# First halves of the first two projection units placed among the second-half modulation products, which use another PSUM bank

## The reference

```python
mod = c @ w_ada + b_ada                                  # c: one prompt row, 8 sample rows
shift, scale, gate = jnp.split(mod[:, None, :], 3, axis=-1)
h = rms_norm(x, norm_g) * (1 + scale) + shift            # (tokens, 1024)
proj = h @ w_in                                          # 3328 columns, split in eight
...                                                      # window attention; HGRN2 recurrence
g_a, g_b = jnp.split(jax.nn.sigmoid(h @ w_merge + b_merge), 2, axis=-1)
y = g_a * (ya @ w_proj_a) + g_b * (yb @ w_proj_b)
out = x + gate * (y @ w_out)
```

## Time and profile before

| | us |
|---|---|
| device time, median of 3 runs | 1617.27 |
| lowest, highest | 1616.54, 1617.92 |
| the profiled execution's own time | 1617.43 |
| its span, first to last instruction | 1614.5 |
| TensorE busy in it | 1564.4 (97%) |
| VectorE, ScalarE, GpSimd busy | 752.2, 555.2, 822.6 |

### The profile page before, as it was taken

One profiled execution on the slowest core, in us unless ns is written; L12 is line 12 of the kernel. 1 busy time (PEld: TensorE's weight loads), 2 busy tenths in 40 slices (PEclk: granted clock), 3 DMA queues, 4 the chain that ended last, 5 costly groups with the idle time before them and its releaser, 6 DMA issues.

```text
span 1614.5 us, 32929 instructions
## 1 busy us (share of the span) xinstructions
PE 1564.4 (97%) x13608; PEld 1268.2 (79%) x13608; DVE 752.2 (47%) x1930; ACT 555.2 (34%) x1131; POOL 822.6 (51%) x1080
## 2 busy tenths in 40 slices
PE   5999999999999999999999999999999999999998
PEld 2787778877888778888879877788888977788886
DVE  3665554233458655532245665623334655623122
ACT  3334323434322432333422343244432344143330
POOL 2425333556673633455756452437777363337671
PEclk9999999999999999999999999999999999999999
DMA  9723112344565321233365331223455331123351
GB/s 321 230 77 93 54 55 66 92 120 129 170 164 124 102 77 51 70 93 117 92 184 132 85 92 54 67 72 115 137 174 156 86 105 54 55 79 91 93 163 67
DMA packets 304971, 175.87 MB, mean 109 GB/s; under 512 B 74158, under 2 KB 290567, under 8 KB 304808
## 3 DMA queue, kind: packets, MB, share of 16 engines
q1 hardware_dynamic: 304824, 173.79, 37.3%
HBM read 159.69 MB, written 11.96 MB: 106 GB/s over the span
## 4 chain that ended last, share of the span: by engine, by line
PE 88%; DVE 6%; issue 2%; ACT 2%; SPq 2%; DMA 1%; POOL 0%; DVEq 0%
PE ps_D L751 50%; PE ps_D L748 24%; PE ps_XD L806 2%; SPq L503 2%; ACT p_or_hf L1107 1%; PE ps_XB L885 1%; PE ps_XA L918 1%; PE ps_XA L907 1%; PE ps_XB L933 1%; PE ps_XA L938 1%; PE ps_XB L932 1%; DMA th_t<-in_w_ada 1%; DVE p_or_hf L1462 1%; PE ps_XC L818 1%; PE ps_XA L885 1%
## 5 line engine op out<-in xcount | busy, mean ns | idle before, releaser
L1650 POOL TENSOR_TENSOR w_lo_t<-w_raw,w_hi_t 128x256 fp32r<-128x256 f32 x928 | 676.9, 764 | 632.1 <-ACT w_hi_t L964 631.8
L751 PE MATMUL ps_D<-h_hi_t,w_hi_t 128*128 128x512 f32 x1024 | 414.9, 405 | 0.1
L751 PE MATMUL ps_D<-h_hi_t,w_lo_t 128*128 128x512 f32 x1024 | 400.4, 391 | 1.2 <-issue 1.2
L751 PE MATMUL ps_D<-h_lo_t,w_hi_t 128*128 128x512 f32 x1024 | 400.8, 391 | 0.0
L964 ACT ACTIVATE w_hi_t<-w_raw 128x1024 fp32r<-128x1024 f32 x232 | 240.2, 1052 | 78.8 <-PE ps_D L748 45.0
L751 PEld LDWEIGHTS ps_D<-h_hi_t,w_hi_t 128*128 128x128 f32 x1024 | 193.0, 188 | 51.9 <-issue 14.8
L751 PEld LDWEIGHTS ps_D<-h_hi_t,w_lo_t 128*128 128x128 f32 x1024 | 192.8, 188 | 42.0
L751 PEld LDWEIGHTS ps_D<-h_lo_t,w_hi_t 128*128 128x128 f32 x1024 | 193.2, 189 | 36.3 <-issue 0.3
L748 PE MATMUL ps_D<-w_hi_t,h_hi_t 128*128 128x384 f32 (+1 forms) x384 | 141.9, 370 | 3.0 <-issue 1.4
L748 PE MATMUL ps_D<-w_hi_t,h_lo_t 128*128 128x384 f32 (+1 forms) x384 | 136.4, 355 | 1.5 <-issue 1.5
L748 PE MATMUL ps_D<-w_lo_t,h_hi_t 128*128 128x384 f32 (+1 forms) x384 | 136.4, 355 | 0.0
(11 more groups left out here) (390 smaller groups left out, 2373.5 us busy)
## 6 DMA issues: line engine op xcount, KB each, us to landing
w_raw<-in_w_in SPq DMA_DIRECT2D x72, 512.0 KB, 3.9
w_raw<-in_w_merge SPq DMA_DIRECT2D x64, 512.0 KB, 4.0
w_raw<-in_w_in SPq DMA_DIRECT2D x64, 256.0 KB, 3.9
w_raw<-in_w_out SPq DMA_DIRECT2D x32, 512.0 KB, 4.1
x_or_AT<-in_x_prompt SPq DMA_DIRECT2D x20, 512.0 KB, 5.2
w_raw<-in_w_proj_a SPq DMA_DIRECT2D x64, 128.0 KB, 3.0
w_raw<-in_w_proj_b SPq DMA_DIRECT2D x32, 256.0 KB, 3.2
xr<-in_x_prompt SPq DMA_DIRECT2D x16, 512.0 KB, 4.8
```

What stands on the lines that cost most here:

```text
L751: ins = mm(bank[:, :], w[:, s0, k0 + k, :], a[:, k, :], start=go, stop=end)
L1650: ins = g_.tensor_tensor(w_lo[:, c, k:k + 2], w_raw[:, n % NRAW, k:k + 2], f32(w_hi[:, c, k:k + 2]), ALU.subtract)
```

## The change

Parts 0 and 1 of the second half of the modulation products stay where they are. Then comes half 0 of unit 0, part 2, half 0 of unit 1, and part 3. The loop over units leaves these two halves out; its side work stays. Because half 0 of unit 1 writes bank D1, the modulation products of the second half that wrote D1 now write XC. XC held the turned sample rows, so these are copied to `hS` first (one new instruction on VectorE), and TensorE waits for the copy (`p_hS`) ahead of the second half. No product is added or taken away.

```diff
-            def ada_half(h):
-                for p in range(4):
+            def ada_part(h, parts):
+                for p in parts:
...
-                    for n, b in (((0, "D0"), (2, "XC")), ((1, "D1"), (3, "XD")))[h]:
+                    for n, b in (((0, "D0"), (2, "XC")), ((1, "XC"), (3, "XD")))[h]:
...
-            ada_half(0)
+            ada_part(0, range(4))
...
             s.wait_ge("p_vec", 1)
-            ada_half(1)
-            s.wait_ge("p_rows", 4)
-            turn_rows(1)
+            s.wait_ge("p_hS", 1)
...
+            ada_part(1, (0, 1))
+            dense(0, 0, 0)
+            ada_part(1, (2,))
+            dense(0, 1, 0)
+            ada_part(1, (3,))
+            s.wait_ge("p_rows", 4)
+            turn_rows(1)
             for it in range(NIT):
                 for u in range(NU):
                     for hf_ in (0, 1):
-                        dense(it, u, hf_)
+                        if it or u > 1 or hf_:
+                            dense(it, u, hf_)
...
-            s.done(fn(mod_rows[:, 512:1024], pb["D1"][:, :], ACT.Copy), "p_rows")
+            s.done(fn(mod_rows[:, 512:1024], XC[:, :], ACT.Copy), "p_rows")
...
+            s.wait_ge("p_T", 3)
+            do(cp(hS[:, :, 0:NS], XC[:, 0:NS * KT].rearrange("p (k b) -> p k b", k=KT)), "p_hS")
             modulation(0)
...
-            do(tt(hS[:, :, 0:NS], XC[:, 0:NS * KT].rearrange("p (k b) -> p k b", k=KT), gscale[:, :, 0:NS],
-                  ALU.mult))
+            do(tt(hS[:, :, 0:NS], hS[:, :, 0:NS], gscale[:, :, 0:NS], ALU.mult))
```

More of the change, by code:

```diff
@@ L247 @@
         + [f"ada{k}" for k in range(2 * KT)] + [f"gw{p}" for p in range(4)]
-        + ["p_late", "p_load0", "p_load1", "p_load2", "p_load3", "p_load4", "p_c", "p_T", "p_xs", "p_mod", "hm", "p_vec", "p_lb", "p_exp0", "p_rows", "p_scale", "p_x2",
+        + ["p_late", "p_load0", "p_load1", "p_load2", "p_load3", "p_load4", "p_c", "p_T", "p_hS", "p_xs", "p_mod", "hm", "p_vec", "p_lb", "p_exp0", "p_rows", "p_scale", "p_x2",
            "p_x3", "p_bg", "fin", "act_step", "dve_step", "pool_step"])
```

## The result

| | before | changed |
|---|---|---|
| median of 8 runs each, in one job | 1616.44 us | 1620.47 us |
| lowest and highest | 1614.6, 1619.19 | 1617.02, 1624.7 |
| ratio, with its 95% interval | | 1.0025 (1.0014 to 1.0035) |
| a second job, 11 and 35 runs | 1616.03 us | 1620.0 us, 1.0019 (1.0011 to 1.0028) |

A forecast was written before the change was run, and what follows sets the result against it. TensorE, busy in 97% of the span, was taken as the bound. Chain 2.9 − 2.29 saved + waits 0.9 and 0.6 = 2.1, plus 1.6 for the clock: 3.7 us, so 1617.43 becomes 1621.1 us; range 1618.6 to 1623.0.

The forecast's parts named there:

- the chain, at half 1 of unit 0: From part 3 through modulation and tiles to half 1 of unit 0: everything 2.9 us late, bounds 2.8 and 3.0.
- half 0 of unit 1 is gone from the stream: Behind the first bursts, TensorE no longer runs this half there: 2.29 us saved.
- wait for D0: Ahead of unit 2: bank D0 free at 59.6, wanted at 58.7, so TensorE waits 0.9 us.
- wait for XD: Ahead of the burst after unit 2: bank XD freed late by ScalarE; 0.6 us in the sum, possibly nothing.
- the clock, over half 1 of unit 0: Clock falls to half speed between 47.5 and 51, costing 1.6 us; possible range from nothing to 3.0.
- The first half takes no time on the path: Half 0 of unit 0 runs beside the chain, costing nothing today; half 0 of unit 1 takes 2.29 us in the stream.
- Part 3 at 43.0: Last part of the modulation products starts at 43.0 instead of 40.11, behind both moved halves and part 2.
- The clock didn't hold: Rival, behind part 3: transposes and narrow products keep the clock up, only waits count, 1619.5 us; chance 0.20.
- part 3 never waited for its load: Rival, at part 3: the `th_t` load lands at 43 or later, hiding both halves, 1615.1 us; chance 0.09.
- nothing was late at 36.85: Rival, at part 2: first half waits for its low part, making part 2 late; called small, no chance of its own.
- the slow stretch ended with half 1 of unit 0: Rival: the clock returns only after transposes and bursts too, 5.1 us in all, 1622.6 us; chance 0.06.
- From 61 on TensorE transmits the delay whole: Behind unit 2 and its burst: no further such wait opens unless one had under 0.7 us slack.

The follow-up runs named there:

- once more: The changed kernel unaltered, for a second profile and more timed runs; ratio 1.0019 to the kernel before.
- hole filled: Changed kernel plus 11 throwaway products behind the second half's narrow products and 4 behind tile 2's transposes; ratio 1.0008 to the kernel before.
- the late chain alone: Changed kernel with 12 throwaway products in place of each moved half, both real halves back where the kernel before has them; ratio 0.9997 to that kernel.
- the bank alone: Changed kernel with its other bank, the copy of sample rows and the wait for it, but no half moved; ratio 0.9998 to the kernel before.
- half 0 of unit 0 alone: Changed kernel with only half 0 of unit 0 moved, ahead of part 2; ratio 1.0013 to the kernel before.
- the two pieces in idle time: Half 0 of unit 1 cut in two, ahead of part 3 and behind tile 2's transposes; first reader order 1.0000, second 0.9983 to the kernel before.
- the best reordering: Half 0 of unit 1 in two pieces, VectorE only freeing D0 and ScalarE reading unit 0 and first bursts ahead of tile 3; 0.9983 to the kernel before.

## Why the prediction was right, point by point

The terms of the sum, with what the starts of the same instructions show in three profiles (us by which TensorE is later than in the kernel before):

| term | forecast | changed | once more | hole filled |
|---|---|---|---|---|
| the chain, at half 1 of unit 0 | 2.9 | 2.76 | 2.67 | 2.77 |
| half 0 of unit 1 is gone from the stream | −2.29 | −2.43 | −2.41 | −2.43 |
| wait for D0 | 0.9 | 1.05 | 1.05 | 1.05 |
| wait for XD | 0.6 | 0.28 | 0.52 | 0.14 |
| the clock, over half 1 of unit 0 | 1.6 | 1.70 | 1.82 | 0.01 |
| sum, at half 1 of unit 3 (0.03 and less come behind the burst) | 3.7 | 3.39 | 3.68 | 1.54 |

- *The first half takes no time on the path, the second 2.29 us.* Right. Alone, the first saves nothing; the second's saving shows once its readers are early. It is 0.1 more than forecast, since the bursts on both sides of it now run as one group.
- *Part 3 at 43.0, the chain 2.9 late.* 42.86 and 42.77. The place is right with luck: the first half went at 36.42 and 36.34, not at 36.85, since the slow stretch around 30 was 3.4 us long in these two profiles and 6.8 in the one before; and the two halves and part 2 took 6.4 us (42.86 − 36.42), not the 6.06 of the sum. With the long stretch, in the late chain alone, part 3 came at 43.21, above my bound of 43.0. The lateness hangs on the landing of `th_t`: with the bank alone changed it came at 39.09, and against such an early landing the loss is larger.
- *Wait for D0, 0.9.* 0.88 in the brackets of both profiles, 1.05 by the starts.
- *Wait for XD, 0.6.* Right in kind; 0.3 and 0.5 in size. In the first profile the term was too high: the load took 4.9, not 5.35, as its lower bound allowed.
- *The clock, 1.6, the term with the widest bounds.* 1.70 and 1.82, read as the length of half 1 of unit 0 (3.89, 4.01) over 2.19. The fall was forecast rightly, between 47.5 and 51 (48.5 and 48.8). The size is near by luck. I took 1.6 as the middle between no loss and 3.0, with 2.2 for a half that is slow throughout. This half was slow throughout (0.50 until 55.3 and 55.6), and that costs 1.7 to 1.8: its products start 0.32 us apart at half speed, not the 0.36 that I got by doubling, and 0.17 at full speed. The filled hole shows for the preamble that it is the want of products. The Trainium skill says in TensorE: Matmul & The Clock Gate, What's actually happening, that activity releases the throttle. The trace agrees: 1.00 from 36 to 70 with the hole filled. What the Trainium skill says of transposes in Part 4 (PE-mode transpose) of the same page was not tested by itself; 8 of them and 16 narrow products did not hold the clock in three profiles of the changed kernel's order.
- *Sum 3.7.* 3.39 and 3.68 in the preamble, 4.0 and 3.1 by the two jobs' ratios, 3.7 between the spans of the second.
- *The rivals.* The clock didn't hold in any of three profiles with this order of products; part 3 never waited for its load in them; nothing was late at 36.85; and the slow stretch ended with half 1 of unit 0.
- *From 61 on TensorE transmits the delay whole.* True of the changed kernel within the intervals, but I had no part of the sum for stops in issue. For a kernel with another number of instructions it is wrong, as the late chain alone showed. Here the numbers are equal (13608 products both), and the issue waits nearly so: 6.3 us before, 6.4 and 5.3 in the changed kernel. Within that, the stop of 1.2 us at 977 is gone in both its profiles, and those at 212 and 240 cost 0.5 to 0.6 us more.
- *"The kernel before doesn't have such a hole".* Too strong. With half 0 of unit 0 left in its place, the clock fell behind part 3 in two of nine profiles, for 3.4 us (at 44.5 with the bank alone, at 45.6 with half 0 of unit 1 alone), and this half took most of it in idle time. With that half moved away and nothing in its place it fell in four of four, for 6.8 us.

## What to carry to other kernels

Before work is moved into an idle time, see whose idle time it is: put ahead of the link on which a chain waits, 4.3 us of products delay the whole chain by what doesn't fit (2.8), and the place that they left, in the chain's shadow, becomes a hole in which the clock may fall. Then follow each buffer that the freed engine will want earlier to its reader; here two readers took back 1.3 and 1.6 us of the 2.4 saved. With the readers moved the wrong way the two pieces in idle time gained nothing (1.0000), and with them moved the right way, in another job, they paid (0.9983). Judge a few us by the start of the same instruction behind the changed stretch, or by spans at a like mean clock, not by the span of one execution, and add no TensorE instructions to a test kernel without counting the stops in issue.

## What was not expected of the hardware

- 24 products of 9 columns whose results are thrown away, issued while TensorE was idle, made the kernel 0.17% faster (0.9983, 0.9972 to 0.9994), with 4.0 us of issue waits in place of 6.3. That is as much as the best reordering gained in the same job.
- Products of 512 columns that write different quarters of the partitions ran side by side: behind part 2 and with its loads landed, part 3 began 0.55 us after it and not 1.8 (39.78 against 39.23, half 0 of unit 0 alone).
- The clock's slow stretches stand at the same places in all fourteen profiles (30, 483, 565, 954 and 1326 here), but which of them an execution has, and for 3.4 or 6.8 us, differs. In the full stream one of 3.4 us is worth up to 1.7 us (1.6 at 483). That is most of the spread of one kernel: the eight spans of the changed kernel in the first job run from 1614.5 at a mean clock of 0.994 to 1622.5 at 0.990.
